# Where GpSimd multiplies in the scan, where step sizes are computed, and attention without loops

## The reference, cut to what matters

```python
u = silu(centred_dwconv(xbc, conv_w, conv_b))          # x, B, C from the projection
dt = softplus(dt_raw + dt_bias)                         # step sizes, 8 heads, 2 directions
acum = cumsum(dt * a)                                   # within a chunk of 128 tokens
decay_to_end = exp(acum[-1] - acum)
chunk_states = einsum(bh * decay_to_end, x * dt)
state = state * exp(acum[-1]) + chunk_states            # chunk after chunk
lmat = exp(where(causal, acum_l - acum_s, -inf))
y_diag = einsum((C @ B) * lmat, x * dt)
y_off = einsum(C, state at chunk start) * exp(acum)
y = y_forward + y_backward + x * d_skip
g = y * silu(z)                                         # then normed and projected
```

## Time and profile before

| what | value |
|---|---|
| median of 3 runs | 3597.33 us (3596.41 to 3608.34) |
| the profiled execution's time | 3598.47 us |
| its span, first to last instruction | 3596.6 us |
| PE busy | 3298.9 us, 92% |
| DVE busy | 1859.5 us, 52% |
| POOL busy | 1366.3 us, 38% |
| ACT busy | 979.0 us, 27% |
| mean granted TensorE clock | 0.955 |
| scan of layer 0, its own step block included | 688.8 to 843.5 us |
| scan of layer 1, the same | 2573.6 to 2697.8 us |

### The profile page before, as it was taken

One profiled execution on the slowest core, in us unless ns is written; L12 is line 12 of the kernel. 1 busy time (PEld: TensorE's weight loads), 2 busy tenths in 40 slices (PEclk: granted clock), 3 DMA queues, 4 the chain that ended last, 5 costly groups with the idle time before them and its releaser, 6 DMA issues. The chain is left out here.

```text
span 3596.6 us, 46435 instructions
## 1 busy us (share of the span) xinstructions
PE 3298.9 (92%) x16876; PEld 2747.4 (76%) x16876; DVE 1859.5 (52%) x2934; ACT 979.0 (27%) x1992; POOL 1366.3 (38%) x967
## 2 busy tenths in 40 slices
PE   5879989888989999999997779989889899999997
PEld 4668878667778888888885659878667688888884
DVE  8777824687673333333226766835695631221225
ACT  4147732342240000000003336742342300000002
POOL 0154222253543334443432144212336545444443
PEclk9979999998999999999998879999999999999998
DMA  8400011002212112221111510011003111111111
GB/s 324 157 1 1 0 48 53 12 18 93 66 52 67 58 58 70 69 66 63 41 35 60 210 47 1 1 46 52 9 18 129 48 47 52 48 51 47 47 52 47
DMA packets 70340, 212.65 MB, mean 59 GB/s; under 512 B 6608, under 2 KB 17616, under 8 KB 69328
## 3 DMA queue, kind: packets, MB, share of 16 engines
q1 hardware_dynamic: 58752, 178.59, 14.9%
q10 hardware_dynamic: 11472, 32.53, 2.6%
HBM read 191.70 MB, written 19.40 MB: 59 GB/s over the span
## 5 line engine op out<-in xcount | busy, mean ns | idle before, releaser
L201 PE MATMUL ps<-h_hi,f_whi 128*128 128x512 f32 (+1 forms) x1760 | 650.4, 370 | 3.5 <-DVE f_gated L2758 3.5
L202 PE MATMUL ps<-h_lo,f_whi 128*128 128x512 f32 (+1 forms) x1760 | 648.4, 368 | 0.0
L203 PE MATMUL ps<-h_hi,f_wlo 128*128 128x512 f32 (+1 forms) x1760 | 647.9, 368 | 0.0
L2758 DVE TENSOR_TENSOR f_gated<-f_gated,ps 128x512 f32<-128x512 f32 (+1 forms) x110 | 69.6, 634 | 818.1 <-PE ps L203 816.8
L2584 POOL TENSOR_TENSOR f_whi<-f_wraw,small 128x1024 fp32r<-128x1024 f32 x130 | 247.8, 1906 | 560.4 <-PE ps L203 529.8
L2767 DVE SCALAR_TENSOR_TENSOR x_res<-ps,mod,x_res 128x512 f32<-128x512 f32 (+1 forms) x440 | 306.6, 697 | 242.9 <-PE ps L203 242.6
L201 PEld LDWEIGHTS ps<-h_hi,f_whi 128*128 128x128 f32 x1760 | 332.3, 189 | 60.9 <-DVE f_gated L2758 3.9
L202 PEld LDWEIGHTS ps<-h_lo,f_whi 128*128 128x128 f32 x1760 | 332.3, 189 | 55.7 <-issue 1.0
L203 PEld LDWEIGHTS ps<-h_hi,f_wlo 128*128 128x128 f32 x1760 | 332.0, 189 | 55.4
L2586 POOL TENSOR_TENSOR f_wlo<-f_wraw,f_whi 128x1024 fp32r<-128x1024 f32 x130 | 326.1, 2509 | 10.2
L201 PE MATMUL ps<-f_ahi,f_whi 128*128 128x512 f32 (+1 forms) x880 | 328.2, 373 | 0.6 <-DVE x_res L2767 0.6
(11 more groups left out here) (269 smaller groups left out, 6544.8 us busy)
## 6 DMA issues: line engine op xcount, KB each, us to landing
f_wraw<-in_w_ffn SPq DMA_DIRECT2D x130, 512.0 KB, 3.5
ada_w<-in_w_ada SPq DMA_DIRECT2D x80, 512.0 KB, 4.6
later_w<-in_w_ada ACTq DMA_DIRECT2D x32, 512.0 KB, 3.5
o_wraw<-in_w_out SPq DMA_DIRECT2D x28, 512.0 KB, 3.5
wrawc<-in_w_in SPq DMA_DIRECT2D x26, 512.0 KB, 4.0
wrawab<-in_w_in SPq DMA_DIRECT2D x16, 512.0 KB, 4.8
x_res<-x_spill SPq DMA_DIRECT2D x6, 1024.0 KB, 7.9
x_res<-in_xT SPq DMA_DIRECT2D x8, 640.0 KB, 7.3
```

What stands on the lines that cost most here:

```text
L201: pe.matmul(out, w_hi, h_hi, start=first, stop=False)
L202: pe.matmul(out, w_hi, h_lo, start=False, stop=False)
L203: return pe.matmul(out, w_lo, h_hi, start=False, stop=last)
L2758: dve.tensor_tensor(g, g, pl.bank(3 + c, tn), ALU.mult).then_inc(u_taken[c], 1)
```

## The change

Five edits:

1. `over_units` writes all attention blocks out; loops, register-held counts and addresses go. In `score` the wait for `p_done` goes, and `values` leaves out the waits for copies that the score two units on already waited for (`awaited`).
2. `project_ssd` takes the dt block first and one z block last. The step sizes are computed there: DVE's chain right after the dt block is stored, ACT's exponentials and logarithm after block 1, the five sums on PE after block 3's transposes. The last z block is stored to DRAM at the end of the stage, and the stage waits for that transfer.
3. `scan` loses its first block. DVE clears `hb` and `hf` at the start of the main block.
4. POOL's four products of chunk o wait for `hf_done >= o`, that is, until DVE has added the state of chunk o - 1, and for nothing else.
5. PE's `segments(1)` stands behind all nine backward states; the first step of `hb` and of `hf` is a copy from PSUM, not a product and a sum.

The core of the diff:

```diff
-    segments = [(0, 1), (1, 2), (2, 6), (6, 7), (7, 8)] + ...
-    def over_units(eng, body):
-        for lo, hi in segments:
-            if hi - lo > 1:
-                with eng.Fori(lo, hi) as b:
-                    for h in range(HEADS):
-                        body(Unit(lo, b, h))
+    def over_units(body):
+        for b in range(len(blocks)):
+            for h in range(HEADS):
+                body(Unit(b, b, h))
...
-                if not (w.static and w.u < 2):
-                    pe.wait_ge(p_done, w.u - 1)
...
-                wait_copied(w, g)
+                if g > awaited(w):
+                    wait_copied(w, g)
...
-    kinds = ["z"] * 4 + ["x"] * 4 + ["b"] * 2 + ["s"] * 2 + ["dt"]
+    kinds = ["dt"] + ["z"] * 3 + ["x"] * 4 + ["b"] * 2 + ["s"] * 2 + ["z"]
+    sums = (((AFTER, dend, FW), (BEFORE, dend, BW), (UPTO, eac, FW)),
+            ((FROM, eac, BW), (ONES, cdec, slice(0, 2 * CH))))
+    STEP_AT = 3
...
             over(sp, segments, chunks_of, body)
+            z_store(12)
             sp.wait_ge(z_out, 64)
...
-                if o < TT - 1:
-                    if o >= 2:
-                        pool.wait_ge(q["st_full"], o - 1)
+                if o >= 1:
+                    pool.wait_ge(q["hf_done"], o)
+                if o < TT - 1:
                     pool.tensor_tensor(heads(xfe[s][:, :]), x, per_head(wde, c, FW), ALU.mult) \
...
-                if y >= 2:
-                    pool.wait_ge(q["diag_full"], y - 1)
...
-                if y >= 2:
-                    pool.wait_ge(q["y4"], y - 1)
...
                 if o == 3:
                     segments(0)
                     products(0)
-                if o == 5:
-                    segments(1)
+            segments(1)
...
+                if o == 0:
+                    dve.wait_ge(q["st_full"], 1)
+                    dve.tensor_copy(hf[1][:, :], pl.bank(4)).then_inc(q["hf_done"], 1)
+                    dve.wait_ge(q["hf_done"], 1)
+                    return
```

More of the change, by code:

```diff
@@ L998, in turned_bank, with awaited @@
             return 3 * self.par + (2 - g if self.kind == "A" else g)
-    def over_units(eng, body):
-        for lo, hi in segments:
-            if hi - lo > 1:
-                with eng.Fori(lo, hi) as b:
-                    for h in range(HEADS):
-                        body(Unit(lo, b, h))
-            else:
-                for h in range(HEADS):
-                    body(Unit(lo, lo, h))
+    def over_units(body):
+        for b in range(len(blocks)):
+            for h in range(HEADS):
+                body(Unit(b, b, h))
+    def awaited(v):
+        w = v.step(2)
+        if w is None:
+            return -1
+        banks = {3 * w.par + (place + int(w.kind == "A")) // 4 for place, _, _ in w.runs()}
+        return max([g for g in range(len(groups[v.kind])) if v.turned_bank(g) in banks], default=-1)
     final = Unit(len(blocks) - 1, len(blocks) - 1, HEADS - 1)
@@ L1026, in _ @@
                 pool.memset(raw(q_pad[p0:p0 + HD, h0:h0 + 2, :]), 0.0).then_inc(q_ready, 1)
-            for lo, hi in segments:
+            for b in range(len(blocks)):
                 def stage(b):
-                    g = blocks[lo][2]
+                    g = blocks[b][2]
                     i = b - g * tiles
@@ L1049, in stage @@
                             .then_inc(q_ready, 1)
[L1050 to L1054, removed]
+                stage(b)
         @block.tensor
@@ L1076, in score @@
                 for place, tile, n in w.runs():
-                    if not (w.static and w.u < 2):
+                    if w.u >= 2:
                         v = w.step(-2)
@@ L1226, in body @@
                     output(last_but_one)
-                if w.static and w.u == 0:
+                if w.u == 0:
                     split_keys(1)
@@ L1238, in exponent @@
                 act.wait_ge(nm_done, w.u + 1)
-                if not (w.static and w.u < 2):
+                if w.u >= 2:
                     act.wait_ge(t_full, w.step(-1).all)
-                if not (w.static and w.u < HEADS):
+                if w.u >= HEADS:
                     act.wait_ge(o_done, w.u - (HEADS - 1))
@@ L1313, in project_ssd @@
     z_out = pl.sem(f"{tag}_z_out")
+    FW, BW = slice(0, CH), slice(CH, 2 * CH)
+    dt, dta, eac, cdec, wde = pl.dt, pl.dta, pl.eac, pl.cdec, pl.wde
+    dend, biased, size, decay, log1 = (pl.at(f"{tag}_step{d}", [P, TT, 2 * CH], F32, kb=80 + 0.625 * d)
+                                       for d in range(5))
+    av = pl.at(f"{tag}_av", [P, 2 * CH], F32, kb=84)
+    step, acted = pl.sem(f"{tag}_step"), pl.sem(f"{tag}_acted")
+    sums = (((AFTER, dend, FW), (BEFORE, dend, BW), (UPTO, eac, FW)),
+            ((FROM, eac, BW), (ONES, cdec, slice(0, 2 * CH))))
+    STEP_AT = 3
     turns = {n: [] for n in range(13)}
@@ L1320, in project_ssd @@
             turns[n] = [(of, c) for c in order_of(kinds[of])]
+        if n == STEP_AT:
+            turns[n] += [("sum", j) for j in range(len(sums))]
     flat = [x for n in range(13) for x in turns[n]]
@@ L1366, in body @@
                     q = number[of, c]
+                    if of == "sum":
+                        pe.wait_ge(step, 10)
+                        pe.wait_ge(stored, q + 1)
+                        for j, (m, _, _) in enumerate(sums[c]):
+                            mm = pe.matmul(pl.bank(6 + q % 2)[:, TT * 2 * CH * j:TT * 2 * CH * (j + 1)], pl.c(m),
+                                           dta[:, :, :].rearrange("p t h -> p (t h)"), start=True, stop=True)
+                        mm.then_inc(turned, 1)
+                        continue
                     if kinds[of] in ("z", "dt"):
```

166 lines of the change are left out of this document (83 added, 83 removed).

## The result

The changed kernel takes 3545.86 us (median of 4 runs, 3541.31 to 3549.92) against 3596.87 for the kernel before in the same session: ratio 0.9849, 95% interval 0.9834 to 0.9864. The direction was right, the size was not. The profiled execution has a span of 3542.8 us, 53.8 less than before.

The account below looks back on a forecast made before the run. PE was taken to bound attention and projection, DVE the scan, small step operations the gap between. Savings of 6.0 + 5.8 + 7.5 - 3.0 + 8.0 + 0.5 + 3.8 + 3.0 = 31.6 us gave 3566 us, range 3553 to 3577.

Parts of the forecast that it names:

- Attention's B pairs: Attention's looped B blocks: written out, 24 pairs save 0.25 us each, 6.0 us in all (0 to 16).
- A blocks: Attention's A blocks: no gain from writing them out, because PE is already full there.
- The projection's end: Between projection and scan: 5.8 us saved in layer 0 and 7.5 in layer 1, 13.3 together.
- the cost inside it: Projection: the five sums now on a full PE cost 1.5 us per layer, 3.0 in all.
- the clock in layer 0's scan: Front of layer 0's scan: earlier upper clock gives 1.0 us (0 to 3) of 8 saved (4 to 11).
- the costing of GpSimd's products by full periods at full clock: Scan loop: products behind the chunk's state save 0.85 us per full period, 3.8 in layer 0, 3.0 in layer 1.
- the pause of 2.97 us: Front of layer 0's scan: PE's wait for the state on DVE at 735.47 goes, saving 2.97 us.
- the period: Scan loop: falls from 11.35 to 10.5 us, set by DVE; PE without its wait needs 10.3.
- the five: Rivals: attention gives nothing, 3572; attention faster, 3556; POOL's products gain nothing, 3575; straight code slower, 3626; projection's end costlier, 3574.
- Rival (2): Attention: all blocks fall to the pace of the last block, 10 us more saved, 3556 us; chance 0.15.

Follow-up runs that it names:

- the filler: The kernel before with five thrown-away 128x512 matmuls in layer 0 between offsets(0) and products(1), filling TensorE's 2.97 us pause; ratio 0.9993 (0.9978 to 1.0007).

## Why the prediction was too small, step by step

**Right.** Attention's B pairs (6.0 forecast, 8.2 here): right mechanism, the size a quarter short. I took the pace of the one straight block as the goal, 8.30 for a pair; with all blocks straight it is 8.26, and the loops' borders and that straight block gain too. A blocks gave nothing by the change; layer 0's A part differs by 1.9 us between executions of either kernel (100.1 or 102). The projection's end (13.3 forecast, 13.6 measured) and the cost inside it (3.0 forecast, 2.3 measured) hold. Only the split of the latter is another: 0.8 us in the matmuls, 1.5 us ahead of the first one.

**Wrong, first: the clock in layer 0's scan.** The step that failed reads: "with fewer pauses PE's clock should reach its upper level earlier than it did, which I put at 1.0 more (0 to 3)", together with the costing of GpSimd's products by full periods at full clock, 3.8 us for layer 0. Measured: 2.95 us of the front are the segments alone (6.55 to 3.60). In the loop the first two periods gave 6.6 us of the 12.9 that all eight gave, where I had 1.5 for them; by the filler 3.8 of these are the clock. And I tied the clock to the wrong part. The moved segments take out one pause, and the clock falls in the next; the pause of 2.97 us, which I booked as gone by the segments' move, stays at 2.24 with it and goes to 0.44 with GpSimd's waits. Parts of one change were costed apart, and what joined them was TensorE's state.

How much of this the kernel before pays differs between its executions, and some of the surplus is therefore luck of the trace that I compared with. The run with two loads swapped in the output projection has the scan of the kernel before unchanged. Its clock fell at other moments:

```profile
719.94 3.70 PE L1638 MATMUL ps<-s_up,const 128*128 128x512 f32 x8 [3.60 <-ACT s_up L1726]
...
736.64 0.71 PE L1651 MATMUL ps<-c_feat,b_feat 128*128 128x128 f32 x4 [2.02 <-DVE s_hf L1795]
```

Behind the same pause of 3.60 us the segments took 3.70 us instead of 6.55, the first period was 12.74 instead of 14.28, and the scan took 136.7 us from first product to last mix instead of 141.2. Against that trace the change would have saved 4.5 us less in layer 0's scan. The other traces whose scan of layer 0 has no pause taken out (attention alone, step sizes alone, GpSimd held in the output projection) have 141.5 to 143.5 us.

**Wrong, second: the period.** I took DVE for 10.5 us (both L1812 and L1815 blocked by 0.85 each) and 10.3 as TensorE's floor. It is 10.03. DVE lost 0.1 and 0.73 (0.56 and 0.73 when TensorE is made faster), and TensorE's gap was 1.2 us where its row said 1.05, with another 0.1 between products and diagonal. Against the 10.5 us that I forecast, 0.47 us a period is 2 to 3 us in layer 0.

The Trainium skill ("SBUF — State Buffer", SBUF: two separate sides) has the port as an exclusive lock for a whole instruction, held by whoever starts first. This trace agrees, and I applied it too coarsely: the price of a meeting is what is left of the other's instruction, between 0.1 and 0.85 us here, not all of it.

**Wrong, third: a stage that the sum left out.** The output projection's 7.3 us were in no term, because I read only the stages that the diff touches. They belong to the attention part by a side way: undoing that part alone lengthens the stage to 163.7 us and costs 16 to 20 us, twice the 8.2 that attention itself gives. But the gain is luck of timing, not of attention: two swapped loads or one wait give it to the kernel before as well. It cannot be read from the trace of before how far the weights will be shifted; that the stage stood a few tenths of a microsecond from a 7 us gain could: twelve divisions of 10.82 us, in a line that takes 3.24 us for the same twelve when alone, and TensorE waiting 8.27 us for them.

**The rivals.** None of the five was the case. Rival (2) is the nearest in time (3556) and wrong in place. All five moved a term; none asked whether the granted clock behind a pause belongs to the pause's price. My range fell short by that and by the output projection: with the 11.7 us of front and loop in the sum its middle would have been 3554, and with the output projection's 7.3 us as well 3547, near the measured 3545.9.

## What to carry to other kernels

A pause of TensorE costs its length and, when the clock falls with it, what runs at the lower clock behind it: read the granted clock in the window after each pause that a change removes, and price the slow instructions there too, as a range, since the same pause was followed by 3.70 and by 6.55 us for the same eight matmuls in two executions. Ask which engine's lateness makes the pause, and who blocks that engine; a wait that moves a blocker once only moves the pause. And where two engines meet at a port by chance, a stage that the diff never touches can move by 7 us: look for instructions that take a multiple of their own best time anywhere in the kernel, and set a wait there so that the outcome does not hang on tenths of a microsecond.

## What the runs showed of the hardware

The loop with the old waits idles TensorE for 1.05 us ahead of the products in its full periods, and for 1.43 or 1.44 us behind each period of 12.35 us. That mostly passes at full clock. Now and then the clock falls behind the longer of these pauses, and the next two periods are 12.7 and 12.35 instead of 11.36 us each. It happened in layer 1 of the run with attention alone:

```profile
2612.00:2624.00 12.00, 10.56 (x47) 8.26 (x47) 11.34 (x17) 5.22 (x20) 3.77 (x4) 0.72 0.12 29
2624.00:2636.00 12.00, 12.00 (x63) 8.79 (x62) 8.14 (x12) 6.66 (x22) 5.62 (x5) 1.00 0.05 18
```

It was there too in the runs with segments alone, the filler, GpSimd held in the kernel before, and the changed kernel with old waits. Kernels with all the new waits and all matmuls, whose loop has next to no pause of TensorE, show no 12.7 us period in any trace. The Trainium skill ("TensorE: Matmul & The Clock Gate", HAM oscillation — how this bites in real kernels) describes such swings in a kernel whose TensorE waits for DMA between bursts of matmuls, so that each burst starts slow. These traces agree as to the swing, though the pauses here (1.4 to 3.6 us) are waits for DVE, GpSimd or ACT, not for DMA. The swing would explain part of the wider spread of the kernel before (3587 to 3609 us) against the changed one (3540 to 3550), which is argued from these traces and was not tested by itself.
